# One inference step of a hybrid RWKV-7 and differential-attention layer: the turned attention weights moved by one engine, and the stage behind the recurrence cut by token thirds

## The reference, cut to what matters

```python
s = einsum("bqhd,bkhd->bhqk", q, k) * 64 ** -0.5      # causal
p = softmax(s).reshape(b, 4, 2, tq, tk)
w = p[:, :, 0] - lam * p[:, :, 1]
o = einsum("bhqk,bkhd->bqhd", w, v)
```

```python
y = (y - mu) * rsqrt(var + eps) * ln_w + ln_b
y = (y + sum(r * k * r_k) * v) * g            # g = sigmoid(gd) @ w_g2
o = rms_norm(o, da_subln) * (1 - lam_init)
merged = g_a * (y @ w_proj_a) + g_b * (o @ w_proj_b)
```

## Time and profile before

| what | value |
|---|---|
| median of 3 runs | 2872.41 us (2867.37 to 2874.47) |
| the profiled execution's own time | 2871.94 us |
| its span, first to last instruction | 2870.1 us |
| PE busy, DVE busy, ACT busy | 2728.9, 1378.8, 655.6 us |
| mean granted TensorE clock | 0.965 of full |

### The profile page before, as it was taken

The page is one execution under the profiler, slowest core; times in us unless marked ns, Lnnn a source line. Parts: engine busy times, 40 slices in busy tenths (PEclk is TensorE's granted clock), DMA queues, the critical chain, the costliest instruction groups (busy, mean ns, idle before and its releaser), DMA issues.

```text
span 2870.1 us, 52015 instructions
## 1 busy us (share of the span) xinstructions
PE 2728.9 (95%) x21467; PEld 2576.9 (90%) x21467; DVE 1378.8 (48%) x1461; ACT 655.6 (23%) x1006; POOL 268.4 (9%) x258
## 2 busy tenths in 40 slices
PE   6999999999999999997776999889999999999998
PEld 6999999999999999997343899759999999999998
DVE  4332233223575588767666687555443322332333
ACT  4111111112311222232333222211221101110223
POOL 1000000000001132113000554200000000000000
PEclk7999999999999999998898999869999999999999
DMA  3111111111233445668755000123211111111112
GB/s 104 44 46 50 44 51 44 52 44 40 99 96 107 145 144 179 204 207 297 253 163 148 29 25 29 44 89 125 74 45 49 46 52 44 44 52 44 44 42 76
DMA packets 270206, 252.12 MB, mean 88 GB/s; under 512 B 20724, under 2 KB 216144, under 8 KB 269920
## 3 DMA queue, kind: packets, MB, share of 16 engines
q1 hardware_dynamic: 252960, 189.42, 22.2%
q0 software_dynamic: 16896, 60.40, 5.7%
q10 hardware_dynamic: 192, 0.07, 0.0%
HBM read 209.93 MB, written 39.90 MB: 87 GB/s over the span
## 4 chain that ended last, share of the span: by engine, by line
PE 88%; DVE 7%; ACT 1%; issue 1%; DMA 1%; SPq 1%; DVEq 0%; POOL 0%; ACTq 0%; POOLq 0%
PE ps L1756 73%; PE ps L2066 1%; PE ps L2081 1%; DVE small L1474 1%; PE ps L1800 1%; PE ps L2086 1%; PE ps L2277 1%; PE ps L1963 1%; DMA value_ring<-in_cache_v 1%; PE ps L1920 1%; PE ps L2113 1%; PE ps L1986 1%; PE ps L2121 1%; PE ps L2009 1%; PE ps L2025 0%
## 5 line engine op out<-in xcount | busy, mean ns | idle before, releaser
L1756 PE MATMUL ps<-h_hi,w_hi 128*128 128x344 f32 x3072 | 992.2, 323 | 10.3 <-DVE w_lo L1196 10.3
L1756 PE MATMUL ps<-h_lo,w_hi 128*128 128x344 f32 x3072 | 981.1, 319 | 0.0
L1756 PE MATMUL ps<-h_hi,w_lo 128*128 128x344 f32 x3072 | 980.7, 319 | 0.0
L1756 PEld LDWEIGHTS ps<-h_hi,w_hi 128*128 128x128 f32 x3072 | 578.2, 188 | 25.9 <-issue 19.8
L1756 PEld LDWEIGHTS ps<-h_lo,w_hi 128*128 128x128 f32 x3072 | 578.4, 188 | 2.1 <-issue 1.9
L1756 PEld LDWEIGHTS ps<-h_hi,w_lo 128*128 128x128 f32 x3072 | 578.3, 188 | 0.0
L1756 PE MATMUL ps<-ff_hi,w_hi 128*128 128x344 f32 x1056 | 337.1, 319 | 0.0
L1756 PE MATMUL ps<-ff_lo,w_hi 128*128 128x344 f32 x1056 | 336.6, 319 | 0.0
L1756 PE MATMUL ps<-ff_hi,w_lo 128*128 128x344 f32 x1056 | 336.2, 318 | 0.0
L833 ACT ACTIVATE w_hi<-w_stage 128x1024 fp32r<-128x1024 f32 x194 | 203.8, 1051 | 480.3 <-PE ps L1756 480.3
L1196 DVE TENSOR_TENSOR w_lo<-w_stage,w_hi 128x1024 fp32r<-128x1024 f32 x194 | 239.2, 1233 | 139.2 <-ACT w_hi L833 103.7
(11 more groups left out here) (405 smaller groups left out, 3282.4 us busy)
## 6 DMA issues: line engine op xcount, KB each, us to landing
w_stage<-in_ffn_up SPq DMA_DIRECT2D x176, 256.0 KB, 3.1
key_ring<-in_cache_k SPq DMA_DIRECT2D x128, 256.0 KB, 3.0
value_ring<-in_cache_v SPq DMA_DIRECT2D x128, 256.0 KB, 3.0
w_stage<-in_w_in SPq DMA_DIRECT2D x84, 256.0 KB, 3.3
w_stage<-in_ffn_down SPq DMA_DIRECT2D x80, 256.0 KB, 2.9
gate_save<-tmp POOLq DMA_DIRECT2D x16, 516.0 KB, 4.5
gate_ring<-gate_save POOLq DMA_DIRECT2D x16, 516.0 KB, 4.4
row_ring<-row_save SPq DMA_DIRECT2D x40, 128.0 KB, 3.0
```

Source lines behind the costliest of these rows:

```text
L1756: last = mm(dense[s][:, j], w[w0][:, k0 + k, :], r[:, k, j * CH:(j + 1) * CH], start=(k == 0 and n == 0), stop=(k == nk - 1 and n == 2))
```

## The change

In the attention, ACT moves the turned weights of a step in one instruction of `n` columns over both banks, after `w_trans_hi`; DVE's move and its wait are gone, and so is PE's wait for it between the fourth and the fifth transpose. Steps under 16 do what they did.

Behind the recurrence a part is now one third of the tokens for all four head tiles (four matmuls, one to a bank), in the order bonus, inverse root, gate, attention's root. The bonus needs neither root nor reciprocal, so its first part waits only for the copied rows. `ya_hi`, `ya_lo`, `yb_hi`, `yb_lo` are made by thirds, and the o result goes to a tile of its own (`y_bonus`) instead of `tmp`.

```diff
 # ScalarE
                 act.wait_ge(*ev.at("w_trans_lo", step + 1))
-                lo = min(4, qi + 1) * P
-                sc.activation(wT[s][:, 0:lo], PS[:, 4, 0:lo], ACT.Copy).then_inc(ev["w_lo_moved"], 1)
+                if step >= FIRST:
+                    act.wait_ge(*ev.at("w_trans_hi", step + 1 - FIRST))
+                n = (qi + 1) * P
+                sc.activation(wT[s][:, 0:n], PSf[:, 4 * 512:4 * 512 + n], ACT.Copy).then_inc(ev["w_moved"], 1)
...
-            for h in range(HP):
-                act.wait_ge(*ev.at("y_used", 3 * h + 3))
-                sc.activation(YA[0][:, h, :], CUM[:, h, :], ACT.Copy).then_inc(ev["ya_high"], 1)
+            for j in range(NCH):
+                b = third_of(j)
+                act.wait_ge(*ev.at("y_used", 2 * NCH + j + 1))
+                sc.activation(YA[0][:, :, b], CUM[:, :, b], ACT.Copy).then_inc(ev["ya_high"], 1)
 # VectorE
-                if qi >= 4:
-                    dve.wait_ge(*ev.at("w_trans_hi", step + 1 - 4 * HP))
-                    in_turn(v.tensor_copy(wT[s][:, 512:n], PS[:, 5, 0:n - 512]).then_inc(ev["w_hi_moved"], 1))
...
+            for j in range(NCH):
+                b, bonus = third_of(j), spread_at(j)
+                in_turn(v.tensor_tensor(ybonus[:, :, b], Vf[:, :, b], bonus, ALU.mult).then_inc(ev["y_used"], 1))
+            for j in range(NCH):
+                b, root = third_of(j), spread_at(NCH + j)
+                for h in range(HP - 1):
+                    in_turn(v.scalar_tensor_tensor(CUM[:, h, b], CUM[:, h, b], param("rw_ln_w", h), root[:, h], ALU.mult, ALU.mult))
...
+                in_turn(v.tensor_tensor(CUM[:, :, b], CUM[:, :, b], ybonus[:, :, b], ALU.add))
 # TensorE
-                    if t == 4 and step > 4 * HP:
-                        pe.wait_ge(*ev.at("w_hi_moved", step - 4 * HP))
...
-            pe.wait_ge(*ev.at("wkv_made", 1))
-            pe.wait_ge(*ev.at("y_inverse", NC))
-            for part in range(3 * HP):
-                h, kind = divmod(part, 3)
-                if part >= 2:
+            pe.wait_ge(*ev.at("ck_rows_in", NC))
+            for part in range(4 * NCH):
+                kind, j = divmod(part, NCH)
+                first, b = part % 2 * HP, third_of(j)
+                if part == 1:
+                    pe.wait_ge(*ev.at("wkv_made", 1))
+                if 2 <= part < 3 * NCH + 2:
                     pe.wait_ge(*ev.at("y_used", part - 1))
-                if part == 0:
+                if part == NCH:
                     pe.wait_ge(*ev.at("y_root", 1))
```

More of the change, by code:

```diff
@@ L1679, in _, with spread_at @@
[L1679 to L1687, removed]
-                        .then_inc(ev["yb_split"], 1))
+            def spread_at(part):
+                dve.wait_ge(*ev.at("y_parts", part + 1))
+                return PS[:, part % 2 * HP:part % 2 * HP + HP, 0:CH]
@@ new lines, in _ @@
+            for j in range(NCH):
+                b, gate = third_of(j), spread_at(2 * NCH + j)
+                for h in range(HP - 1):
+                    in_turn(v.scalar_tensor_tensor(CUM[:, h, b], CUM[:, h, b], param("rw_ln_b", h), gate[:, h], ALU.add, ALU.mult))
+                in_turn(v.scalar_tensor_tensor(CUM[:, HP - 1, b], CUM[:, HP - 1, b], param("rw_ln_b", HP - 1), gate[:, HP - 1],
+                                               ALU.add, ALU.mult).then_inc(ev["y_used"], 1))
+                if j:
+                    ya_low(j - 1)
@@ new lines, in _ @@
+            for j in range(NCH):
+                b, scale = third_of(j), spread_at(3 * NCH + j)
+                for h in range(HP - 1):
+                    in_turn(v.scalar_tensor_tensor(ybonus[:, h, b], Q[:, h, b], param("da_subln", h), scale[:, h], ALU.mult, ALU.mult))
+                in_turn(v.scalar_tensor_tensor(ybonus[:, HP - 1, b], Q[:, HP - 1, b], param("da_subln", HP - 1), scale[:, HP - 1],
+                                               ALU.mult, ALU.mult).then_inc(ev["yb_full"], 1))
+                if j == 0:
+                    ya_low(NCH - 1)
+                else:
+                    yb_low(j - 1)
@@ L1690, in _ @@
+            yb_low(NCH - 1)
             split(0, AT_MERGE)
@@ L2267, in _ @@
                     pe.wait_ge(*ev.at("y_used", part - 1))
-                if part == 0:
+                if part == NCH:
                     pe.wait_ge(*ev.at("y_root", 1))
-                if part == 2:
+                if part == 2 * NCH:
                     pe.wait_ge(*ev.at("g2_loaded", 16))
                     pe.wait_ge(*ev.at("gd_back", 16))
-                q = slice(32 * h, 32 * h + 2)
-                for j in range(NCH):
-                    cols = slice(j * CH, (j + 1) * CH)
-                    if kind < 2:
-                        last = mm(dense[part % 2][:, j], K("row_heads")[q], Rf[q, kind, cols], start=True, stop=True)
-                    else:
-                        last = mm(dense[part % 2][:, j], G2[:, h * P:(h + 1) * P], gd[:, cols], start=True, stop=True)
@@ L2291, in _ @@
-            pe.wait_ge(*ev.at("ya_split", HP))
+                if part == 3 * NCH:
+                    pe.wait_ge(*ev.at("o_root", 1))
+                if part == 4 * NCH - 1:
+                    pe.wait_ge(*ev.at("yb_full", 1))
+                for h in range(HP):
+                    out, q = PS[:, first + h, 0:CH], slice(32 * h, 32 * h + 2)
+                    if kind == 0:
+                        last = mm(out, K("row_heads")[q], Rf[q, 1, b], start=True, stop=True)
+                    if kind == 1:
+                        last = mm(out, K("row_heads")[q], Rf[q, 0, b], start=True, stop=True)
+                    if kind == 2:
+                        last = mm(out, G2[:, h * P:(h + 1) * P], gd[:, b], start=True, stop=True)
+                    if kind == 3:
+                        last = mm(out, K("ones")[32 * h:32 * h + 1], rmix[32 * h:32 * h + 1, b], start=True, stop=True)
```

76 lines of the change are left out of this document (34 added, 42 removed).

## The result

| what | before | after |
|---|---|---|
| median of 6 runs each | 2869.24 us (2866.75 to 2874.47) | 2845.68 us (2836.64 to 2851.72) |
| ratio after to before, 95% interval | | 0.9908 (0.9892 to 0.9924) |
| span of the profiled execution | 2870.1 us | 2846.7 us |
| the first merge product starts at | 1917.16 us | 1893.55 us |

The change makes the kernel 23.6 us faster, 0.9%. Everything behind the merge's first product takes what it took in the two profiles (953.0 us before, 953.2 after), so their whole difference was made ahead of it.

A forecast was written before the change was run, and what follows sets the result against it. PE, busy for 95% of the span, was taken as the bound, with DVE's chain beside it in the touched stages. Attention 12.4, clock 2 and stage 1.2 gave 15.6 us off 2871.94, about 2857 us, range 2847 to 2867.

The forecast's parts named there:

- The 24 row products of the first six parts: Behind the recurrence: PE takes 1.19 us each at 1.2 GHz, 1.15 without a gap, 27.5 us in all.
- the bound that I gave to PE in this half: First six parts behind the recurrence: PE needs 4.6 us a part, DVE keeps up with 4.3 us.
- The first part started right behind the copy: Start of the stage behind the recurrence: at about 1857.15 and not 1859.39, 2.2 us gained.
- The clock rose within the gate products: Behind the recurrence: twelve gate products stand together, the clock should rise within them, and DVE becomes the bound.
- my 1.2: Stage behind the recurrence: 0.4 us earlier by the sum, up to 1.7 more if the clock is high; 1.2 us taken.
- The attention: Late attention steps: 12.7 us saved over 15 steps, less 0.3 us in the last step, 12.4 us.
- full steps: Attention steps 18, 21, 23, 24 and 29: DVE's wait and copy saved in full, 7.5 us together.
- PE's list: Attention steps with sums: PE's own work sets 9.2 us against 9.54; 16, 19, 22 and 25 save 0.2 us each.
- The clock term: Attention: with PE denser, one stretch at 1.2 GHz goes away, 2 us saved, bounds 0 and 5 us.
- The copy of the last step: Last attention step: ACT's longer copy, which nothing hides, costs 0.3 us.
- Rival 2: Attention's low clock all gone (7 us), stage gains 3 us with DVE at the page's price: 2849 us, chance 0.12.
- Rival 4: Attention: one-piece copy makes PE wait longer before values, 4.8 us, and the clock falls more, 4.4 us: 2881 us, chance 0.05.

The follow-up runs named there:

- same_group: The changed kernel with every row product reading rows 0 and 1 (attention's root row 0) whatever its head: 2855.00 us, 0.9958 of the kernel before, stage 59.0 us.
- late_start: The changed kernel with the first bonus part again waiting for the state's copy, reciprocal and root: 2848.51 us, 0.9932 of the kernel before, stage 48.8 us.
- stage_only: The changed kernel with the attention's part undone, only the stage behind the recurrence changed: 2856.98 us, 0.9956 of the kernel before, stage 47.2 us.
- before_spread: The kernel before, in its old order, with row products of a part's three thirds reading three row groups: 2852.67 us, ratio 0.9947, stage 45.6 us.
- att_only: The changed kernel with the stage behind the recurrence undone, only the attention changed: 2861.02 us, 0.9972 of the kernel before, stage 60.6 us.
- fold: The changed kernel with factors folded into the spreading rows, so DVE has fewer, longer products: 2833.69 us, 0.9884 of the kernel before, stage 40.9 us.
- two_groups: The changed kernel with a part's four row products reading rows of only two row groups: 2850.81 us, 0.9931 of the kernel before, stage 49.4 us.

## Why the prediction was wrong in its size

**The step that failed** is the term "The 24 row products of the first six parts take 7.14 / 6 = 1.19 us each at 1.2 GHz" and the 27.5 us of PE that follow from it. That price belongs to products of one row group, one behind the other. In the old order the three products of a part share the two rows of one head; in the new order the four products of a part read partitions 0, 32, 64 and 96 and write four banks, and run beside each other: 1.60 us a part, 0.40 a product at 1.2 GHz. The six parts kept PE busy for 8.1 us (0.86 and 0.96 us for the first two, at or near full clock, then 1.53 to 1.6 us each), not 27.5. The Trainium skill has this in "TensorE: Matmul & The Clock Gate", section "Part 3: Packing small matmuls — row/col tiling": small products whose operands start in different groups of 32 partitions run concurrently, and four with 32 rows and 512 columns measured 3.07 times as fast. The trace agrees: 4.65 / 1.60 = 2.9 times here, in same_group against the change.

So the bound that I gave to PE in this half was DVE's: by my own prices its work on the six parts is 3 x 1.68 + 3 x 4.3 = 17.9 us, and it took 1866.45 - 1848.58 = 17.9.

I used a duration of a shape ("2*128 2x344") as if the shape fixed it. The earlier trace rows could have told otherwise. At full clock a lone 344-column product takes 0.6 us (half of 1.19), 1.7 ns per column; the four score products in the earlier trace rows, whose operands lie in two halves of 64 partitions, take 1.78 us for two of 512 and two of 384 columns (the row names only the wider), 1.0 ns per column; the eight value products in the earlier trace rows, whose outputs lie in four groups of 32, take 1.90 us, 0.46 ns per column. That is about two and four at once. All these neighbours of different row groups write different banks, and no run put two of them into one bank, so whether they need that is not shown.

**What followed from it.** With PE at 27.5 us the gate part would reach DVE 32.5 us behind the start; it did 1866.45 - 1846.68 = 19.8 us behind. That is 12.7 us of the 12.8 by which the stage was shorter than forecast (60.0 and 47.2 us). From there to the merge I had 27.2 us of DVE, and it was 1893.55 - 1866.45 = 27.1 us. The first part started right behind the copy, as said, and late_start gives 1.6 us for it. The clock rose within the gate products (full from 1866.4 to 1876.6 us), as said. It was low again at the merge: the first ten to twelve MATMUL of the merge take 0.4 to 0.6 us each before and after, and 0.32 us once the clock is full, and the 0.8 us of my 1.2 that stood for a high clock there did not come.

**The attention was right in its sum, and partly by luck.** The distances between the transposes of one step and the next, in us: before is the median of three profiles with the old attention (before, stage_only, before_spread), after that of six with the new one (after, att_only, same_group, late_start, fold, two_groups).

| step | 16 | 17 | 18 | 19 | 20 | 21 | 22 | 23 | 24 | 25 | 26 | 27 | 28 | 29 | 30 | sum |
|---|---|---|---|---|---|---|---|---|---|---|---|---|---|---|---|---|
| before | 7.13 | 8.70 | 7.12 | 8.38 | 7.98 | 8.32 | 8.82 | 8.52 | 8.77 | 9.53 | 14.96 | 10.59 | 9.58 | 9.75 | 9.57 | 137.7 |
| after | 6.71 | 8.70 | 6.08 | 8.29 | 6.80 | 7.02 | 9.22 | 8.54 | 7.22 | 9.06 | 13.74 | 8.22 | 8.31 | 7.96 | 9.11 | 125.0 |
| saved | 0.42 | 0 | 1.04 | 0.09 | 1.18 | 1.30 | -0.40 | -0.02 | 1.55 | 0.47 | 1.22 | 2.37 | 1.27 | 1.79 | 0.46 | 12.7 |
| predicted | 0.2 | 0 | 1.15 | 0.2 | 1.1 | 1.40 | 0.2 | 1.40 | 1.64 | 0.2 | 0 | 1.0 | 1.2 | 1.89 | 1.0 | 12.6 |

(The predicted steps add up to 12.6; I had rounded to 12.7.) The full steps 18, 21, 24 and 29 save 0.1 us less than their price each, 20 and 28 come as forecast, and 16, 19 and 25 save 0.1 to 0.5 us, near the 0.2 that I gave for PE's list. 27 saves 1.4 us more and 30 half a us less than predicted, 26 saved 1.2 where I gave nothing. Step 23 shows 7.22 and 7.23 us in two of the six profiles, 1.3 saved, and 22 shows 8.42 or 8.43 in three, 0.4 saved: the medians there hold stretches at 1.2 GHz. That the two sums agree is in part luck: 26 and 27 gave 2.6 us more than I said, and 22, 23 and 30 2.6 us less.

**The clock term is not borne out, and its sign stays open.** I took 2 us off for a denser PE. Between the transposes of step 16 and those of step 31 the granted clock was at 1.2 GHz for 18.8, 19.8 and 12.7 us in the three profiles with the old attention, and for 17.9, 19.4, 11.2, 6.8, 6.8 and 13.6 us in the six with the new, in the order named above: less on average, but profiles of one kind differ by more than the two kinds do. Against the shortest that each step shows in any profile of its kind (sum 136.3 and 121.3 us) the old lose 3.4 us on average and the new 6.5. That is no price of the clock: the shortest of six lies lower than the shortest of three, and waits for pages are in it (step 20 takes 10.41 us in late_start, and 2.5 of these PE waits for a page). In the change's own profile step 22 takes 13.12 us, with PE busy for 9.85 of 10.2 us at 0.51. The mean sums are 139.7 and 127.8: the attention gave 11.9 us in its steps, where 14.7 were forecast with the clock; the whole of att_only gave 8.0 (4.9 to 11.5). The copy of the last step, 0.3 us, is too small to be told in a stretch that ends 58.7 to 61.1 us behind those transposes. Why the stretches at 1.2 GHz fall where they do stays open; they fell at other times in every profile, and the runs after the change spread over 15 us where before spread over 8.

**The sum anew**: 11.9 + 13.2 = 25 us, beside 23.6 measured between medians and 26.4 by the ratio. Rival 2 had about the right time (2849) for a wrong reason: it took 7 us for low clock that would go, and 3 us in the stage by a cheaper DVE; the clock's part is not shown, and the scalar_tensor_tensor of 344 columns took 0.572 us, the 0.58 of the rows. Rival 4's wait is there (15.0 us for the copies in 15 steps, 9.8 in the same steps before), and is covered in the full steps.

## What to carry to other kernels

The duration of a small matmul is no property of its shape alone: ask which partitions its operands start at, and what stands beside it in the queue. When an edit reorders small products, write down for each neighbour pair the row group and the bank, and look in the trace for a group of products that already runs at twice or four times the rate per column. Once such a stage belongs to VectorE, fewer and longer instructions there are the next gain (6.4 us of 47.2 here): factors per partition can ride in the rows that a product spreads.

## What the runs showed of the hardware that was not expected

- Products with 2 rows in one, two and four groups of 32 partitions: 4.65, 2.48 and 1.60 us for four fp32 products of 344 columns at 1.2 GHz, 0.86 us for four groups at 2.4 GHz.
- Such products did not bring the clock up: PE was busy with them without a gap for 26.5 us in same_group, at 1.07 us and more each, while 20 idle-time products of 128 rows and 168 columns had it at 2.4 GHz for the merge's first product. The two cases differ in rows, columns and surroundings at once, so this is an observation, not a separated cause.
